# Two-block transformer kernel: the last value unit of the delta stage is projected between the Gram groups, and its conv rows move into the buffer of the first inverse products

## The reference, cut to what matters

```python
def c_mixer(h, w_in, conv_w, a_log, dt_bias, head_gain, w_out):
    qkv, gate, b, a = _split(h @ w_in, C_SIZES)
    qkv = jax.nn.silu(short_conv(qkv, conv_w))        # causal, 4 taps, 3072 channels
    q, k, v = _split(qkv, (GDN_QK, GDN_QK, GDN_VW))   # 8 heads of 128 each
    ...
    o = gated_deltanet(q, k, v, beta, log_alpha)
    o = rmsnorm(o, head_gain) * jax.nn.silu(gate...)
    return o.reshape(B, T, GDN_VW).astype(h.dtype) @ w_out

def gated_deltanet(q, k, v, beta, log_alpha):
    ...
    kk = jnp.einsum('nbhtd,nbhsd->nbhts', kc, kc)                      # Gram matrix of the keys
    lower = jnp.where(strict, bc[..., :, None] * kk * decay, 0.0)
    sol = lax.linalg.triangular_solve(lower + eye, rhs, ...)           # the inverse
    attn = jnp.einsum('nbhtd,nbhsd->nbhts', qc, kc) * decay
    ...
```

## Time and profile before

| quantity | value |
|---|---|
| median of three runs | 1299.62 us |
| the profiled execution, its time | 1300.14 us |
| the profiled execution, its span | 1298.4 us |
| TensorE busy | 1261.5 us, 97% of the span |
| VectorE, ScalarE, GpSimd busy | 789.2, 706.0, 129.4 us |
| mean granted TensorE clock | 0.995 |

### The profile page before, as it was taken

One profiled execution on the slowest core, in us unless ns is written; L12 is line 12 of the kernel. 1 busy time (PEld: TensorE's weight loads), 2 busy tenths in 40 slices (PEclk: granted clock), 3 DMA queues, 4 the chain that ended last, 5 costly groups with the idle time before them and its releaser, 6 DMA issues.

```text
span 1298.4 us, 22051 instructions
## 1 busy us (share of the span) xinstructions
PE 1261.5 (97%) x9160; PEld 1144.5 (88%) x9160; DVE 789.2 (61%) x1175; ACT 706.0 (54%) x1114; POOL 129.4 (10%) x146
## 2 busy tenths in 40 slices
PE   6999999999999999999999999999999999999997
PEld 6988899998889888898999888988998898999886
DVE  6786678885457656655554447787646545655444
ACT  6766666655467545645555336554355644655433
POOL 6000001110000000000111000105600000111000
PEclk9999999999999999999999999998999999999999
DMA  9533455655545424533655554533203535455550
GB/s 330 178 115 113 146 182 176 195 171 193 177 165 203 162 98 162 189 136 101 196 190 192 193 174 156 177 118 102 93 2 114 195 130 162 153 175 192 195 195 33
DMA packets 142758, 205.52 MB, mean 158 GB/s; under 512 B 3778, under 2 KB 119874, under 8 KB 142658
## 3 DMA queue, kind: packets, MB, share of 16 engines
q1 hardware_dynamic: 142658, 204.11, 47.6%
HBM read 203.05 MB, written 1.05 MB: 157 GB/s over the span
## 4 chain that ended last, share of the span: by engine, by line
PE 86%; DVE 7%; ACT 4%; issue 2%; POOL 1%; DMA 0%; DVEq 0%; SPq 0%; ACTq 0%
PE ps L310 42%; PE ps L372 27%; PE ps L390 5%; DVE weights_lo L289 2%; PE ps L2123 2%; PE ps L2185 1%; PE ps L1747 1%; PE ps L1769 1%; PE ps L526 1%; ACT weights_hi L286 1%; DVE split_arena L557 1%; POOL arena L2411 1%; ACT normed L943 1%; PE ps L794 0%; PE ps L2031 0%
## 5 line engine op out<-in xcount | busy, mean ns | idle before, releaser
L289 DVE TENSOR_TENSOR weights_lo<-weights,weights_hi 128x1024 fp32r<-128x1024 f32 x379 | 470.7, 1254 | 247.4 <-ACT weights_hi L286 245.4
L310 PE MATMUL ps<-split_arena,weights_hi 128*128 128x256 f32 x3056 | 560.2, 286 | 7.3 <-DVE split_arena L557 5.6
L286 ACT ACTIVATE weights_hi<-weights 128x1024 fp32r<-128x1024 f32 x379 | 396.7, 1056 | 253.7 <-PE ps L372 183.0
L310 PEld LDWEIGHTS ps<-split_arena,weights_hi 128*128 128x128 f32 x3056 | 477.7, 192 | 16.0 <-issue 12.9
L310 PE MATMUL ps<-split_arena,weights_lo 128*128 128x256 f32 x1528 | 432.9, 283 | 0.0
L310 PEld LDWEIGHTS ps<-split_arena,weights_lo 128*128 128x128 f32 x1528 | 293.6, 192 | 0.0
L372 PE MATMUL ps<-weights_hi,split_arena 128*128 128x512 f32 x992 | 272.7, 392 | 2.4 <-ACTq L1920 1.6
L372 PEld LDWEIGHTS ps<-weights_hi,split_arena 128*128 128x128 f32 x992 | 184.5, 188 | 41.7 <-issue 2.9
L372 PE MATMUL ps<-weights_lo,split_arena 128*128 128x512 f32 x496 | 153.6, 390 | 0.0
L372 PEld LDWEIGHTS ps<-weights_lo,split_arena 128*128 128x128 f32 x496 | 93.1, 188 | 19.6
L1928 POOL TENSOR_TENSOR normed<-normed 128x512 f32<-128x512 f32 x32 | 34.1, 1066 | 484.4 <-ACTq L1920 484.4
(11 more groups left out here) (375 smaller groups left out, 1310.3 us busy)
## 6 DMA issues: line engine op xcount, KB each, us to landing
weights<-in_mlp_w SPq DMA_DIRECT2D x64, 1024.0 KB, 5.3
weights<-in_w_up SPq DMA_DIRECT2D x22, 1024.0 KB, 5.1
weights<-in_c_w_in SPq DMA_DIRECT2D x16, 1024.0 KB, 5.5
weights<-in_w_in SPq DMA_DIRECT2D x13, 1024.0 KB, 6.7
weights<-in_ab_w_in SPq DMA_DIRECT2D x12, 1024.0 KB, 5.3
weights<-in_w_down SPq DMA_DIRECT2D x11, 1024.0 KB, 4.9
weights<-in_xa_wv SPq DMA_DIRECT2D x8, 1024.0 KB, 4.9
weights<-in_xa_wq SPq DMA_DIRECT2D x8, 1024.0 KB, 5.3
```

The lines of the kernel that those rows point to most:

```text
L286: act.activation(h, r, ACT.Copy).then_inc(s_hi, 1)
L289: dve.tensor_tensor(l, r, h.bitcast(F32), ALU.subtract).then_inc(s_lo, 1)
L310: mm = pe.matmul(o, w[:, k, :], x[:, k, :], start=(k == 0 and i == 0), stop=(k == DC - 1 and i == 2))
```

## The change

The value unit 11 leaves its place ahead of the Gram groups, and a gate unit takes that place in the ring and on TensorE. The weights' order becomes unit 10, gate 1, unit 11, gates 2 and 3; `GP0` stays the same part number. `GP0` and `GP0+1` are now gate 1, `GP0+2` and `GP0+3` unit 11. Unit 11 goes to bank 0, and its conv rows to `YI[:, 0]`, which the first inverse products use only later. TensorE's order is now: gate 1 first part, `gate_columns`, products 0, gate 1 second part, products 1, products 2, unit 11 first part, products 3, unit 11 second part, `blocks` of level 0, and on as before.

```diff
-            cols("c_v", "c_w_in", [2560, 2816])
-            cols("c_gate", "c_w_in", range(3328, 4096, 256))
+            cols("c_v", "c_w_in", [2560])
+            cols("c_gate1", "c_w_in", [3328])
+            cols("c_v1", "c_w_in", [2816])
+            cols("c_gate", "c_w_in", range(3584, 4096, 256))
...
+        def conv_rows(u):
+            return CC[:, u % 4, :, :] if u < 11 else YI[:, 0, :, :].rearrange("p a b -> p (a b)").rearrange("p (c n) -> p c n", c=2)
+
+        def conv_bank(u):
+            return PS[:, G + (u % 4 if u < 11 else 0), :]
...
-            free(11)
-            cols_part(first_unit["c_v"] + 1, 0, HT, G + 3)
+            pe.wait_ge(named("c_conv"), 10)
+            cols_part(first_unit["c_gate1"], 0, HT, 1)
             gate_columns()
-            cols_part(first_unit["c_v"] + 1, 1, HT, G + 3)
...
                 elif n == 2:
-                    pe.wait_ge(named("c_conv"), NCU)
+                    pe.wait_ge(named("c_conv"), 11)
...
                 elif f == 0:
-                    pe.wait_ge(named("c_conv"), 11 - u)
+                    pe.wait_ge(named("c_conv"), NCU)
...
-                pe.wait_ge(named("c_silu"), NCU)
+                pe.wait_ge(named("c_silu"), 11 if gi < 2 else NCU)
...
             products(0)
+            cols_part(first_unit["c_gate1"], 1, HT, 1)
             products(1)
             products(2)
-            gate_part(2)
+            cols_part(first_unit["c_v1"], 0, HT, 0)
             products(3)
-            gate_part(3)
+            cols_part(first_unit["c_v1"], 1, HT, 0)
...
-            for u in range(NCU):
+            def taps(u):
+                cols_done(act, *unit_at(u))
...
+            for u in range(NCU - 1):
...
-            silu(NCU - 1)
+            silu(NCU - 2)
             act.preload_act_table_set(EXP_LN)
...
-                act.wait_ge(s_used, GP0 + 2 * u + 2)
+                act.wait_ge(s_used, GP0 + 2 * u + (2 if u > 1 else 0))
...
-            decays(0)
-            decays(1)
-            decays(2)
-            split(act, GP0 + 5)
-            decays(3)
             act.wait_ge(named("c_row"), 3)
             act.activation(GE[:, :, :], GCB[:, :, 32:72], ACT.Exp).then_inc(named("c_log"), 1)
             act.activation(GX[:, 1, :], GX[:, 0, :], ACT.Exp).then_inc(named("c_log"), 1)
             act.wait_ge(named("c_log"), 6)
+            decays(0)
+            gate_evac(1)
+            split(act, GP0 + 3)
+            decays(1)
+            split(act, GP0 + 4)
+            decays(2)
+            split(act, GP0 + 5)
+            decays(3)
+            taps(NCU - 1)
             split(act, GP0 + 6)
-            gate_evac(1)
+            silu(NCU - 1)
+            act.wait_ge(named("c_silu"), NCU)
+            act.preload_act_table_set(EXP_LN)
             decays(4)
...
-            pool.wait_ge(named("c_silu"), NCU)
+            pool.wait_ge(named("c_silu"), 11)
...
-            conv(NCU - 1)
...
             exponents(0)
+            split(dve, GP0 + 3)
+            decayed(0)
             exponents(1)
-            decayed(0)
+            split(dve, GP0 + 4)
+            decayed(1)
             exponents(2)
-            decayed(1)
+            split(dve, GP0 + 5)
+            decayed(2)
             exponents(3)
-            decayed(2)
             decayed(3)
-            split(dve, GP0 + 5)
+            conv(NCU - 1)
             split(dve, GP0 + 6)
```

## The result

The changed kernel takes 1305.72 us in the median of six runs (1304.78 to 1306.29); the kernel before, on the same chip, takes 1300.55. The ratio is 1.0036, with a 95% interval of 1.0026 to 1.0045: slower by 3.4 to 5.9 us, 5.2 by the two medians. The forecast was +6.0, 1305.6 us. The profiled execution has a span of 1303.1 us against 1298.4, 4.7 more.

The account below looks back on a forecast made before the run. Level 1 on TensorE was taken as bound by GpSimd's masks; c_prep 4 5.7 us later, shorter masks and the lower clock put its end +6.0 us later: 1299.62 + 6.0 = 1305.6 us, range 1302.4 to 1308.2.

Parts of the forecast that it names:

- TensorE's order wins next to nothing: TensorE's reordered work before level 0 wins back only the 0.2 us wait for a conv.
- The start of the row: ScalarE evacuates gate 1 at 884.2, starts split +3 at 884.7; VectorE starts exponents 1 at 887.8.
- The rounds: Exponents, decays, both engines' splits and decayed take 4.77 us a round, so c_prep 4 comes at 900.1, 5.7 us later.
- The masks behind it: GpSimd's six masks after c_prep 4 take 8.85 us, about 0.85 us less for meeting one split fewer.
- Rival 2: Unit 11's conv slows four GpSimd masks by 3.4 us, total about +7.5 us; chance 0.05.
- The clock: TensorE's lower clock lasts 8.1 us from the level 0 restart, until 911.9, slowing level 0, products 4 and part of level 1.
- rival 1: Clock returns during level 0, +4.0 us, or only in gate part 4, +8.0; chance 0.80 together with the forecast.
- The sum: Level 1 on TensorE ends at 913.2 instead of 907.15, +6.0 us, making 1305.6 us.
- Nothing gives time back later: From level 1 on the chain is TensorE's, so the +6.0 us shift stays constant.
- Table loads and weights cost nothing: Two added ScalarE loads lie in idle time (2.6 us uncovered); weight loads up to 5.4 us later also cost nothing.
- Rival 3: Round trips are hidden, c_prep 4 at 894.1, masks done at 902.9: -1.2 us; chance 0.12 with the cases between.

Follow-up runs that it names:

- e3: Changed kernel with gate 1's evacuation on ScalarE moved from behind decays 0 to behind decays 3; 1302.98 us against 1300.27 before, ratio 1.0022.
- e4: Kernel before, unit 11 unmoved, with splits +3, +4, +5 added between exponents and decayed of groups 0 to 2; 1310.63 us against 1300.27, ratio 1.0075.
- e1: Changed kernel with splits +3 and +4 moved ahead of exponents 0, +5 on VectorE into unit 11's conv; 1301.74 us against 1300.27 before, ratio 1.0005.
- e2: Changed kernel with splits +3 and +4 ahead of exponents 0, split +5 left between exponents 2 and decayed 2; 1300.85 us against 1300.27 before, ratio 1.0006.
- e9: Changed kernel with two more table loads on ScalarE ahead of decays 4; 1304.22 us against 1300.60 before, ratio 1.0028.
- e5: Changed kernel with 64 throwaway matmuls added in TensorE's wait before level 0; 1305.36 us against 1300.60 before, ratio 1.0029.
- e6: Kernel before with 18 throwaway matmuls added in TensorE's 2.39 us wait before level 0; 1300.95 us against 1300.60, ratio 1.0004.

## Why the forecast was right, point by point

- **TensorE's order wins next to nothing.** Right: its work ends at 904.33 - 8.27 = 896.06, 17.83 of stage time, before at 18.42; 0.6 us won in place of the 0.2 forecast, and lost again in the wait.
- **The start of the row.** Forecast: evacuation at 884.2, split at 884.7, exponents 1 at 887.8. Measured less 1.10: 884.03, 884.52, 887.57. e3 shows that this head is worth 1.8 of the 5.3 us that the masks start late.
- **The rounds.** Forecast 4.77 us, measured 4.75 in the changed kernel and in e4. `c_prep` 4: forecast 900.1, 5.7 late; measured 899.98 + 0.70, less 1.10, 899.6. e1, e2 and e4 show that the rounds do this and the unit's place doesn't.
- **The masks behind it.** Forecast 8.85 us, measured 8.81. One delay fewer by a split, as worked out. VectorE's timeline, after:

```profile
900.93 2.22 DVE L291 TENSOR_TENSOR weights_lo<-weights,weights_hi 128x1024 fp32r<-128x1024 f32 x1 [0.25 <-ACT weights_hi L288]
903.08 2.67 DVE L2470 SCALAR_TENSOR_TENSOR arena<-ps,cconv_cols,arena 128x255 f32<-128x255 f32 x6
```

The split started 0.1 us behind the mask of 900.81, which took its full 1.26 us, and ended 1.1 us behind that mask's end; the mask of 902.13 ended 1.1 us behind the split's. Split and second mask took 2.22 and 2.15 us, well over their 1.23 and 1.27. The conv of unit 11, from 903.08 to 905.75, ran beside the mask of 904.36, and neither was slower: 2.67 us for six instructions as for unit 10, 1.27 for the mask. Rival 2 is out. The Trainium skill ("GPSIMD Engine Reference", Specifications) says that GpSimd's SBUF interfaces are shared with VectorE, with contention from VectorE instructions that have two SBUF inputs (or run in a two-port mode). The trace agrees for the split, which has two; the conv has one such input, its other being in PSUM, and no contention shows.
- **The clock.** This is the term that was mis-sized against the profile. "I take 8.1 us again" counts from the restart, as if the fall stood at a fixed distance from it. In the changed kernel's profile the clock fell inside the wait and came back 3.3 us behind the restart, and the part of the sum that stood on it, products 4 and level 1 at the lower clock, fell away: level 1 ended +3.6, near the +4.0 that rival 1 gave for an early return. In e9, with the same work on TensorE, it came back 8.9 us behind the restart and level 1 ended +5.9, as forecast. e5 shows that a full clock gains nothing that the times can tell, not that the lower clock is always free.
- **The sum.** That +6.0 came so near the 5.2 us of the medians is in part luck. The profiled execution has +3.6 in the stage, and 1.1 more from code that the change doesn't touch. Whether the median execution is like it or like e9's isn't shown. The upper end of the range, 1308.2, is also not the sum of its named terms: +8.0 with 1.2 more gives 1308.8.
- **Nothing gives time back later.** Not quite: level 2 ended 4.4 us late and 0.8 us came back by the end of level 4.
- **Table loads and weights cost nothing.** The loads: shown by e9. The later issue of weights was not tested by itself; no wait of TensorE for a weight load shows up in the stage after.
- **Rival 3, not slower.** Out as it was put; but its arithmetic is what e1 ran into: masks' end -0.7 of the -1.2 given. Its decision point (`c_prep` 4 by 895.2) is where e2 sits: 894.3 before, e2 1.04 later, 895.3, time +0.06%.

## What to carry over

When two engines pass work to each other (exponents, exp, multiply), a task that is itself passed between the same two, put between the steps, does not fill a gap: it adds nearly its whole latency on both engines, here 2.09 us a round (4.75 us where e1, without it, has 888.88 - 886.22 = 2.66), for splits of 1.04 and 1.23 us. Do such tasks ahead of the exchange, where their inputs allow, and look for what waits behind it on a third engine; here the cure was partly there, in letting GpSimd take the masks whose inputs were ready first. And before a lower clock is priced, ask what bounds the instructions it slows: as far as they wait for another engine anyway, it is free, and beyond that it costs. Here both cases stand in profiles of the same instructions, so a forecast of one execution needs both.

## What the runs showed of the hardware that I had not expected

- The granted clock came back 8.1 us behind the restart in the kernel before, 3.3 us behind it in the changed kernel after a wait three times as long, and 8.9 us behind it in e9 after the same wait. From fall to return it was 6.8 us in the first two and 13.7 in e9, 10.2 in e3, 17.1 in e4 and 3.4 in e6. The stay at the lower level can't be carried over from one row, from the restart least of all.
- It fell in e1 and e6 behind a first level of 64 by 64 blocks at the full clock, with waits of at most 2.47 us, so keeping TensorE busy in one wait did not hold it.
- A VectorE split and a GpSimd mask that meet take 2.22 and 2.15 us in place of 1.23 and 1.27. The starts and ends fit engines that take turns by whole instruction: the first mask ran its usual time, the split ended 1.1 us behind it, and the next mask 1.1 us behind the split.
